# Block border of a two-block kernel: first attention round's q and k from the residual without its norm, step sizes behind the v unit

## The chip, the cores and the metric

The kernel runs on 1 core of one Trainium2 chip. The metric is the device time of one execution in microseconds (us). The engines are PE (TensorE, matmuls; PEld its weight loads), DVE (VectorE), ACT (ScalarE), POOL (GpSimd) and SP (SyncE, here only the queue of weight loads).

## The reference

Two transformer-like blocks on x of 256 rows and width 1024, all in float32. The first block ends with a feed-forward part that is added to the residual x; the second takes the norm of that sum.

```python
def first_block(x, mem, ...):
    ...
    u = _rmsnorm(x, g_mlp[l]) @ w_ff1[l]
    x = x + jnp.square(jax.nn.relu(u)) @ w_ff2[l]
    return x

def second_block(x, norm_mix_pre_w, w_in, ...):
    h = x
    u = rmsnorm(h, norm_mix_pre_w[layer])        # h * rsqrt(mean(h*h) + eps) * gain
    proj = u @ w_in[layer]
    q, k, v, z, xbc, dt_raw, gate_logits = jnp.split(proj, offsets, axis=-1)
    ... dilated window attention of q, k, v (12 heads of 64)
    ssm = mamba2_mixer(z, xbc, dt_raw, ...)      # dt = softplus(dt_raw + dt_bias)
    ...
    h = h + rmsnorm(mixed, norm_mix_post_w[layer])
    f = rmsnorm(h, norm_ffn_pre_w[layer])
    f = jnp.square(jax.nn.relu(f @ w_up[layer])) @ w_down[layer]
    h = h + rmsnorm(f, norm_ffn_post_w[layer])
    return h
```

The root mean square is one number per row of h, so (h * gain) @ w times that number is the same as the norm @ w.

## The kernel before

**Tiles.** Activations stand turned: feature on the partitions, the 256 rows along the free dimension, so a width of 1024 is 8 tiles of 128x256. Each float32 product is made of three in fp32r: an operand is split into a high part (rounded) and a low part (what is left), and `products` (L236) issues hi x hi, lo x hi, hi x lo for each of 8 tiles. A unit is 256 columns of a weight matrix: two halves of 24 matmuls each, on one PSUM bank. `x_hi` and `x_lo` hold 40 tiles of operands: `H0` is tile 0, `M0` tile 8, `Y0` tile 16; the 32 hidden tiles of the feed-forward part stand from tile `U0` = 8.

**Weight pipeline.** Three slots. SP loads a unit into `raw` when its slot's low part was made; ACT casts `raw` to `w_hi` (L198) when the unit that held the slot before has ended on PE; DVE subtracts to make `w_lo` (L204). Each engine calls `split()` by hand at places in its own program; the units are taken in order.

**Order.** Each engine has its own program, written out by hand, and waits on counters (semaphores). Nothing reorders. The stages are cross, stick, mlstm, gx, gs, gm, out, up, down, and for the second block att (3 rounds of q, k, v), ssm (8 rounds), ga, gq, out2, up2, down2.

**The border.** The down stage is `deep`: 16 units, four for each pair of output tiles. After every fourth DVE adds PSUM to `res` (L1189), ACT squares (`squares`, L642) and DVE adds the two squares of a pair (`pair`, L1135). PE sums each pair over the partitions with a matmul by ones (`norm`, L1390), four in all, after the last unit. ACT makes the inverse root (`inverse(1)`, L652, L653, into `rs_row`), DVE scales `res` by it (`scaled`, L1156), ACT makes the high part times the gain (`high`, L647), DVE the low part (`lower`, L1128), all of it on tiles `H0`. PE's q unit waits for the low parts tile by tile. DVE then makes `thin_lo` (L1208), the low part of the thin columns for the step sizes, and goes on with splits, the copies `evac` (L863) of q and k out of PSUM, and the step sizes.

**Step sizes.** `step_sizes`: PE multiplies the thin columns (L245, 24 matmuls) into bank 4; DVE adds the bias (L1212), ACT takes abs, exp, ln (L699 to L701), DVE makes dt and its running sum (L1215 to L1217). POOL writes the sums to memory for the SSM rounds. `step_columns`: PE turns the rows (L1393), DVE copies them to `dtc` and `acs` (L1221, L1222). `att_logits(0)` on PE waits for that.

Of the kernel before, what the change touches and what calls it, by code (L numbers as in the profile page):

```python
# [14 lines left out]
P = 128  # L15
# [38 lines left out]
H0, M0, Y0 = 0, 8, 16  # L54
YSB, YML, YX = Y0, Y0 + 8, Y0 + 16
# [41 lines left out]
def build(nc, a, out):  # L97

    ctx = ExitStack()
    with ctx:  # L100
# [171 lines left out]

        def rs_row():
            return cells(4096, T)
# [91 lines left out]
        def _(pool):  # L366
# [6 lines left out]
            pool.wait_ge(S("s_lo"), 4)  # L373
# [8 lines left out]
            for j in range(3):  # L382
                need(pool, "a_b", j)
                pool.dma_start(a_bias, a["att_bias"][:, 4 * j:4 * j + 4, :]).then_inc(S("a_bias"), 16)
# [7 lines left out]
        def _(act):  # L392
# [75 lines left out]
            def cross(i, j):  # L468
# [17 lines left out]
                A(rows(x_hi, 2 * j + YX, 2), bank(6, 2, T), ACT.Copy).then_inc(S("c_hi"), 1)  # L486
# [22 lines left out]
            def stick_out(j):  # L509

                act.wait_ge(S("s_y"), j + 1)
                A(rows(x_hi, 2 * j + YSB, 2), bank(7, 2, T), ACT.Copy).then_inc(S("s_hi"), 1)
# [51 lines left out]
            def mlstm_out(j):  # L564

                act.wait_ge(S("m_y"), j + 1)
                A(rows(x_hi, 2 * j + YML, 2), m_hm, ACT.Copy).then_inc(S("m_hi"), 1)
# [44 lines left out]
            def mixed(i, n):  # L612

                act.wait_ge(S("p_used"), n + 2)
                A(rows(x_hi, 2 * i + M0, 2), rows(mix, 2 * i, 2), ACT.Copy).then_inc(S("mix_hi"), 1)
# [28 lines left out]
            def high(src, g, b):  # L644

                for k in (2 * b, 2 * b + 1):
                    A(x_hi[:, H0 + k], src[:, k], ACT.Identity, scale=pc(g, k)).then_inc(S("n_hi"), 1)  # L647
# [69 lines left out]
            def att_out(j):  # L717

                act.wait_ge(S("a_y"), j + 1)
                A(rows(x_hi, 2 * j + YAT, 2), bank(7, 2, T), ACT.Copy).then_inc(S("a_hi"), 1)  # L720
# [4 lines left out]
            split()  # L725
# [52 lines left out]
            def ssm_out(j):  # L778

                act.wait_ge(S("d_yn"), j + 1)  # L780
                A(rows(x_hi, 2 * j + YSS, 2), d_y, ACT.Copy).then_inc(S("d_hi"), 1)
# [41 lines left out]
            for i in range(4):  # L823
# [3 lines left out]
                mixed(i, 16 + i)  # L827
# [22 lines left out]
        def _(dve):  # L850
# [90 lines left out]
            def cross(i, j):  # L941
# [29 lines left out]
                low(2 * j + YX, bank(6, 2, T), "c_hi", j + 1, "c_lo")  # L971
# [31 lines left out]
            for i in range(1, 4):  # L1003
# [7 lines left out]
                low(2 * (i - 1) + YSB, bank(7, 2, T), "s_hi", i, "s_lo")  # L1011
# [48 lines left out]
            def mlstm_gate(j):  # L1060
# [3 lines left out]
                low(2 * j + YML, m_hm, "m_hi", j + 1, "m_lo")  # L1064
# [822 lines left out]
```

## Time and profile before

| | us |
|---|---|
| median of 3 runs | 1271.18 |
| lowest, highest | 1270.01, 1271.70 |
| the profiled execution | 1270.2 |
| its span | 1268.4 |
| PE busy in it | 1223.2 (96%) |
| DVE busy | 809.2 (64%) |
| ACT busy | 659.8 (52%) |
| mean granted clock of PE | 0.989 |

The span runs from the first to the last instruction; the profiled execution's own time is 1.8 us longer. Busy shares are means over all stages. The page of the profile gives per line what an engine did and what ended its waits; the trace gives the same for a stretch, and each start. Matmuls overlap: one of 128x256 is shown with 0.28 us, while the next starts 0.12 us after it. A granted clock of 1.00 is 2.4 GHz, 0.50 is 1.2 GHz.

### The profile page before, as it was taken

To read this page: it belongs to the slowest core of one execution; us is meant where nothing else is said; L and a number is where in the kernel's file an instruction comes from. 1 tells how busy PE (TensorE), PEld (TensorE's weight loads), DVE (VectorE), ACT (ScalarE), POOL (GpSimd) and SP (SyncE) were. 2 spreads that over 40 slices of the span, in tenths; PEclk is the share of its full clock that TensorE was granted. 3 is DMA by queue.
4 is the path that set the end of the run, shared out by engine and by line. 5 is a ranking of instruction groups with operands and counts; after the bars stand their busy time and mean duration, and the time that the engine had idled before them with its cause. 6 is when DMAs were issued, how large, how long until landed. Compare 5 with 4: busy or idle time off the path is not lost.

```text
span 1268.4 us, 22328 instructions
## 1 busy us (share of the span) xinstructions
PE 1223.2 (96%) x9844; PEld 1197.3 (94%) x9844; DVE 809.2 (64%) x890; ACT 659.8 (52%) x764; POOL 10.4 (1%) x23
## 2 busy tenths in 40 slices
PE   7999999999999999999989999999989997999996
PEld 6999999999999999999989999999889997999996
DVE  6665666777655557774446577878874555776443
ACT  6443445677543445553334468878764444545330
POOL 0000000000000000000000000000000000000000
PEclk9999999999999999999999999999999998999998
DMA  8553454555656555556555546555446552556540
GB/s 292 168 162 105 134 163 141 146 152 165 200 172 195 166 166 166 176 190 217 182 167 164 178 118 195 167 153 160 156 156 194 194 172 67 181 185 216 183 134 34
DMA packets 210241, 210.28 MB, mean 166 GB/s; under 512 B 6476, under 2 KB 207564, under 8 KB 210144
## 3 DMA queue, kind: packets, MB, share of 16 engines
q1 hardware_dynamic: 207600, 200.30, 50.0%
q0 software_dynamic: 1968, 7.64, 2.1%
q8 instruction: 78, 1.28, 0.4%
q10 hardware_dynamic: 576, 0.90, 0.2%
q14 instruction: 19, 0.16, 0.0%
HBM read 207.73 MB, written 1.09 MB: 165 GB/s over the span
## 4 chain that ended last, share of the span: by engine, by line
PE 75%; DVE 15%; ACT 7%; issue 1%; DMA 0%; DVEq 0%; ACTq 0%
PE ps L236 68%; DVE w_lo L204 6%; PE ps L1390 5%; DVE arena L1020 4%; ACT w_hi L198 2%; DVE arena L1278 1%; ACT L404 1%; ACT arena L766 1%; PE ps L1393 1%; PE ps L245 1%; DVE res L1162 0%; DVE arena L1156 0%; ACT arena L409 0%; DVE arena L1304 0%; DVE arena L1293 0%
## 5 line engine op out<-in xcount | busy, mean ns | idle before, releaser
L236 PE MATMUL ps<-x_hi,w_hi 128*128 128x256 f32 x2752 | 791.6, 288 | 19.2 <-DVE x_lo L1128 9.0
L236 PE MATMUL ps<-x_lo,w_hi 128*128 128x256 f32 x2752 | 781.3, 284 | 0.0
L236 PE MATMUL ps<-x_hi,w_lo 128*128 128x256 f32 x2752 | 781.2, 284 | 0.0
L204 DVE TENSOR_TENSOR w_lo<-raw,w_hi 128x2048 fp32r<-128x2048 f32 x188 | 430.1, 2291 | 231.1 <-ACT w_hi L198 231.1
L236 PEld LDWEIGHTS ps<-x_hi,w_hi 128*128 128x128 f32 x2752 | 530.4, 193 | 26.8 <-issue 21.8
L236 PEld LDWEIGHTS ps<-x_lo,w_hi 128*128 128x128 f32 x2752 | 530.7, 193 | 0.8
L236 PEld LDWEIGHTS ps<-x_hi,w_lo 128*128 128x128 f32 x2752 | 530.6, 193 | 0.0
L198 ACT CAST w_hi<-raw 128x2048 fp32r<-128x2048 f32 x188 | 355.9, 1899 | 117.6 <-PE ps L236 115.6
L236 PE MATMUL ps<-w_hi,x_hi 128*128 128x256 f32 x240 | 69.1, 288 | 2.5 <-DVE w_lo L204 2.5
L1390 PE MATMUL ps<-arena 128*128 128x256 f32 (+3 forms) x448 | 68.1, 341 | 3.1 <-ACT arena L747 2.6
L236 PE MATMUL ps<-w_lo,x_hi 128*128 128x256 f32 x240 | 67.9, 283 | 0.0
L236 PE MATMUL ps<-w_hi,x_lo 128*128 128x256 f32 x240 | 67.8, 283 | 0.0
L1390 PEld LDWEIGHTS ps<-arena 128*128 128x128 f32 (+2 forms) x448 | 54.1, 169 | 11.7 <-ACT arena L747 3.6
L671 ACT ACTIVATE arena<-ps 128x512 f32<-128x512 f32 x32 | 19.1, 598 | 83.9 <-PE ps L236 83.9
L1020 DVE SCALAR_TENSOR_TENSOR arena<-arena,pcol 128x256 f32<-128x256 f32 x144 | 60.1, 480 | 3.5 <-ACT arena L527 2.7
L1390 PE MATMUL ps<-arena,cst 128*128 128x256 f32 (+1 forms) x184 | 45.2, 376 | 10.6 <-DVE arena L881 6.1
L236 PEld LDWEIGHTS ps<-w_hi,x_hi 128*128 128x128 f32 x240 | 46.0, 192 | 2.7 <-DVE w_lo L204 2.7
L1390 PEld LDWEIGHTS ps<-arena,cst 128*128 128x128 f32 x184 | 31.9, 200 | 15.8 <-issue 6.1
L236 PEld LDWEIGHTS ps<-w_hi,x_lo 128*128 128x128 f32 x240 | 46.0, 192 | 0.0
L236 PEld LDWEIGHTS ps<-w_lo,x_hi 128*128 128x128 f32 x240 | 45.9, 191 | 0.0
L1175 DVE TENSOR_TENSOR arena<-arena 128x512 f32<-128x512 f32 x32 | 22.2, 692 | 36.8 <-ACT arena L671 36.8
L609 ACT ACTIVATE arena<-ps,pcol 128x256 f32<-128x256 f32 x40 | 16.8, 471 | 49.3 <-PE ps L236 47.5
(176 smaller groups left out, 696.5 us busy)
## 6 DMA issues: line engine op xcount, KB each, us to landing
raw<-in_w_in SPq DMA_DIRECT2D x170, 512.0 KB, 4.7
raw<-in_w_ff SPq DMA_DIRECT2D x64, 512.0 KB, 4.5
raw<-in_w_up SPq DMA_DIRECT2D x32, 512.0 KB, 4.7
raw<-in_w_down SPq DMA_DIRECT2D x32, 512.0 KB, 4.4
raw<-in_w_mem_kv SPq DMA_DIRECT2D x16, 512.0 KB, 4.6
raw<-in_w_out SPq DMA_DIRECT2D x16, 512.0 KB, 4.7
raw<-in_w_ssm_proj SPq DMA_DIRECT2D x16, 512.0 KB, 4.6
raw<-in_w_x_proj SPq DMA_DIRECT2D x8, 512.0 KB, 4.5
```

The lines of the kernel that those rows point to most:

```text
L198: nc.scalar.copy(w_hi[:, s], raw[:, s]).then_inc(S(f"w_hi{s}"), 1)
L204: nc.vector.tensor_tensor(w_lo[:, s], raw[:, s], w_hi[:, s].bitcast(FP32), ALU.subtract)\
L236: last = nc.tensor.matmul(dst, l, r, start=start and k == 0 and m == 0, stop=stop and k == nk - 1 and m == 2)
L245: last = nc.tensor.matmul(dst, wt[:, c], xt[:, at + k, :], start=k == 0 and m == 0, stop=k == KT - 1 and m == 2)
L404: act.preload_act_table_set("natural_log_exp_and_others")
L609: last = A(gt[:, c], unit_bank(u)[:, c], ACT.Sigmoid, bias=pc(b_gate, k + c))
L671: A(f, unit_bank(u), ACT.Relu).then_inc(taken(u), 1)
L766: A(d_ec, d_ec, ACT.Exp, scale=-1.0).then_inc(S("d_e"), 1)
L1020: last = stt(dst[:, n], pad[:, n, m:m + T], pc("conv_w" + name, tiles[n] + stride * m), dst[:, n], ALU.mult, ALU.add)
L1175: chain(tt(q, f, bc(rs_row(), 2), ALU.mult))
L1278: tt(d_ec, d_ec, bc(d_cb, 4), ALU.mult).then_inc(S("d_L"), 1)
L1390: return nc.tensor.matmul(o, l, r, start=start, stop=stop)
```

## The change

- In the down stage ACT and DVE also make, after each quarter, the high and low part of the residual times the second block's gain (`high` and `lower` on `res`, tiles `H0`, counters `b_hi`, `b_lo`).
- PE runs the first half of q of the first round on those, then the four sums of squares, the second half of q, and k. q and k come out of PSUM by a multiplication with `rs_row` where they were copied (two `tt` in place of two `evac`).
- The normed parts go to tiles `H2` = 8 and are read from the v unit on. The mixed sums of the second block stand at `M2` = 0 in turn.
- PE's thin products for the step sizes stand between the halves of v, in bank 7; the turning of the step columns between the halves of the next round's q. The wait for the columns goes from the first logits to the first `att_values`.
- On ACT and DVE the split of the v unit stands ahead of the inverse norm and of the scaling. On POOL the first bias table is loaded ahead of the step rows, when the low parts are done.
- The counters of five stages become one pair, `y_hi` and `y_lo`.

DVE from the end of the down stage to the first scaling, before (a quarter's addition is L1189, the pair L1135, the scaling L1156) and after (the same are L1199, L1145, L1166; L205 is `split`):

```order
L1189 TENSOR_TENSOR res<-res,ps 128x512
L1135 TENSOR_TENSOR arena<-arena 128x256
L1156 TENSOR_TENSOR arena<-res,arena 128x512 x2
L1128 SCALAR_TENSOR_TENSOR x_lo<-arena,pcol,x_hi 128x256 x2
L1156 TENSOR_TENSOR arena<-res,arena 128x512
```

```order
L1199 TENSOR_TENSOR res<-res,ps 128x512
L1138 SCALAR_TENSOR_TENSOR x_lo<-res,pcol,x_hi 128x256 x2
L1145 TENSOR_TENSOR arena<-arena 128x256
L205 TENSOR_TENSOR w_lo<-raw,w_hi 128x2048
L1166 TENSOR_TENSOR arena<-res,arena 128x512 x2
L1138 SCALAR_TENSOR_TENSOR x_lo<-arena,pcol,x_hi 128x256 x2
```

Two low parts of the residual and the subtraction of the v unit's weights now stand ahead of the scaling.

DVE from the thin low part to the first logits, before (L863 is `evac`, L1212 to L1217 `step_sizes`, L1221 and L1222 `step_columns`, L1228 the logits' bias) and after (`evac` of q and k is now L1262; `step_sizes` L1225 to L1230; bias L1241):

```order
L1208 TENSOR_TENSOR x_lo<-tab,x_hi 128x320
L204 TENSOR_TENSOR w_lo<-raw,w_hi 128x2048
L863 COPY arena<-ps 128x512
L204 TENSOR_TENSOR w_lo<-raw,w_hi 128x2048
L1212 TENSOR_SCALAR mix<-ps,tab 32x256
L1215 SCALAR_TENSOR_TENSOR mix<-mix 32x256
L1216 TENSOR_SCALAR mix<-mix,small 32x256
L1217 SCALAR_TENSOR_TENSOR mix<-mix 32x256
L863 COPY arena<-ps 128x512
L204 TENSOR_TENSOR w_lo<-raw,w_hi 128x2048
L1221 COPY small<-ps 128x64
L1222 COPY small<-ps 128x64
```

```order
L1221 TENSOR_TENSOR x_lo<-tab,x_hi 128x320
L1262 TENSOR_TENSOR arena<-ps,arena 128x512 x2
L205 TENSOR_TENSOR w_lo<-raw,w_hi 128x2048 x2
L1225 TENSOR_SCALAR mix<-ps,tab 32x256
L1228 SCALAR_TENSOR_TENSOR mix<-mix 32x256
L1229 TENSOR_SCALAR mix<-mix,small 32x256
L1230 SCALAR_TENSOR_TENSOR mix<-mix 32x256
L1241 SCALAR_TENSOR_TENSOR arena<-ps,arena 128x1536
```

Both evacuations and two splits stand ahead of the step sizes, one split went ahead of the scaling, and the column copies went behind the logits.

ACT across the same border, before (L642 square, L652 and L653 inverse root, L647 high parts, L198 split) and after (L652, L662 and L663, L657, L199):

```order
L198 CAST w_hi<-raw 128x2048 x4
L642 ACTIVATE arena<-res 128x512
L652 ACTIVATE arena<-ps,small 128x256
L653 ACTIVATE arena<-arena 128x256
L647 ACTIVATE x_hi<-arena,pcol 128x256 x8
```

```order
L199 CAST w_hi<-raw 128x2048 x4
L657 ACTIVATE x_hi<-res,pcol 128x256 x2
L652 ACTIVATE arena<-res 128x512
L199 CAST w_hi<-raw 128x2048
L662 ACTIVATE arena<-ps,small 128x256
L663 ACTIVATE arena<-arena 128x256
L657 ACTIVATE x_hi<-arena,pcol 128x256 x8
```

The v unit's cast stands between the square and the inverse root.

The diff, cut to its core:

```diff
 H0, M0, Y0 = 0, 8, 16
+H2, M2 = M0, H0
...
+            def bias(j):
+
+                need(pool, "a_b", j)
+                pool.dma_start(a_bias, a["att_bias"][:, 4 * j:4 * j + 4, :]).then_inc(S("a_bias"), 16)
+
+            pool.wait_ge(S("n_lo"), 2 * KT)
+            bias(0)
             pool.wait_ge(S("dt_rows"), 1)
...
-            def deep(dst, done0, stop):
+            def deep(dst, done0, stop, g=None):
...
                         act.wait_ge(S(f"deep{b // 4 % 2}"), b // 8 + done0 + 2)
+                        if g is not None:
+                            high(dst, g, b // 4, H0, "b_hi")
                         squares(dst, b // 4 * 2)
 
             hidden("up", 0)
-            deep(res, 0, 16)
-
-
+            deep(res, 0, 16, "norm_mix_pre_w_2")
+            split()
             inverse(1)
             for b in range(4):
                 act.wait_ge(S("n_t"), b + 1)
-                high(cells(2048, KT, T), "norm_mix_pre_w_2", b)
+                high(cells(2048, KT, T), "norm_mix_pre_w_2", b, H2)
...
             split()
             split()
             step_sizes()
-            split()
             evac(U("att", 0, 2, 3), a_v)
...
                         last.then_inc(S(f"deep{c % 2}"), 1)
+                        if g is not None:
+                            lower(dst, g, c, 0, H0, ("b_hi", "b_lo"))
                         pair(n, c)
...
-            split()
-            evac(U("att", 0, 0, 3), a_q)
+            for n, dst in enumerate((a_q, a_k)):
+                u = U("att", 0, n, 3)
+                finished(dve, u)
+                tt(dst, unit_bank(u), bc(rs_row(), 2), ALU.mult).then_inc(taken(u), 1)
+            split()
             split()
             step_sizes()
-            evac(U("att", 0, 1, 3), a_k)
-            split()
-            step_columns()
             for i in (1, 2):
                 att_logits(i - 1)
                 split()
+                if i == 1:
+                    step_columns()
                 evac(U("att", i, 0, 3), a_q)
...
-            for b in range(4):
-                norm(1, b)
-
...
-                if j == 0:
-                    pe.wait_ge(S("dt_col"), 1)
...
             q, k, v = (U("att", 0, n, 3) for n in range(3))
-            unit(q, H0, lo=("n_lo", KT, 1))
+            half(q, 0, H0, lo=("b_lo", 0, 1))
+            for b in range(4):
+                norm(1, b)
+            half(q, 1, H0)
+            unit(k, H0)
+            half(v, 0, H2, TOK, lo=("n_lo", KT, 1))
             step_sizes()
-            unit(k, H0)
-            half(v, 0, H0, TOK)
-            step_columns()
-            half(v, 1, H0, TOK)
+            half(v, 1, H2, TOK)
             for i in (1, 2):
                 q, k, v = (U("att", i, n, 3) for n in range(3))
                 att_logits(i - 1)
-                unit(q, H0)
-                unit(k, H0)
-                half(v, 0, H0, TOK)
+                half(q, 0, H2)
+                if i == 1:
+                    step_columns()
+                half(q, 1, H2)
+                unit(k, H2)
+                half(v, 0, H2, TOK)
                 att_turn(i - 1)
-                half(v, 1, H0, TOK)
+                half(v, 1, H2, TOK)
+                if i == 1:
+                    pe.wait_ge(S("dt_col"), 1)
                 att_values(i - 1)
```

## Rows read from the trace of the kernel before

**Rows 1.** PE's waits by releaser, 470 to 680 us: total us, times, longest.

```profile
PE ps L236 <- DVE x_lo L1128: 2.9, 1, 2.9
```

**Rows 2.** timeline of PE at the border: start us, us, engine line op, count.

```profile
658.34 0.28 PE L236 MATMUL ps<-x_hi,w_lo 128*128 128x256 f32 x1
658.46 1.46 PE L1390 MATMUL ps<-arena,cst 128*128 128x256 f32 x6
660.52 0.70 PE L1390 MATMUL ps<-arena,cst 128*128 128x256 f32 x2 [0.60 <-DVE arena L1135]
664.11 0.55 PE L236 MATMUL ps<-x_hi,w_hi 128*128 128x256 f32 x1 [2.89 <-DVE x_lo L1128]
...
669.30 0.28 PE L236 MATMUL ps<-x_hi,w_lo 128*128 128x256 f32 x1
...
672.28 0.28 PE L245 MATMUL ps<-x_hi 128*32 128x256 f32 x1
...
675.08 0.28 PE L236 MATMUL ps<-x_hi,w_hi 128*128 128x256 f32 x1
...
683.80 0.43 PE L1393 MATMUL ps<-cst,mix 32*128 32x32 f32 x4
...
687.23 1.68 PE L1390 MATMUL ps<-arena 64*128 64x128 f32 x16
...
703.34 1.36 PE L1393 MATMUL ps<-cst,arena 128*128 128x128 f32 x11
```

**Rows 3.** busy time by stretch: PE, PEld, DVE, ACT, POOL, then granted clock, DMA.

```profile
664.10:668.00 3.90, 3.89 (x17) 3.86 (x18) 3.90 (x10) 3.05 (x9) 0.00 (x0) 0.50 0.00 0
```

**Rows 4.** timeline of DVE at the border, columns as in PE's.

```profile
654.88 2.29 DVE L204 TENSOR_TENSOR w_lo<-raw,w_hi 128x2048 fp32r<-128x2048 f32 x1 [3.47 <-ACT w_hi L198]
658.66 0.69 DVE L1189 TENSOR_TENSOR res<-res,ps 128x512 f32<-128x512 f32 x1 [1.48 <-PE ps L236]
...
662.21 1.29 DVE L1156 TENSOR_TENSOR arena<-res,arena 128x512 f32<-128x512 f32 x2 [1.75 <-ACT arena L653]
...
668.42 0.49 DVE L1208 TENSOR_TENSOR x_lo<-tab,x_hi 128x320 fp32r<-128x320 f32 x1
...
676.69 0.47 DVE L1212 TENSOR_SCALAR mix<-ps,tab 32x256 f32<-32x256 f32 x1
...
679.43 0.68 DVE L1217 TENSOR_TENSOR_SCAN mix<-mix 32x256 f32<-32x256 f32 x1
...
696.57 1.83 DVE L1239 TENSOR_TENSOR arena<-arena,small 128x512 f32<-128x512 f32 x2
```

**Rows 5.** timeline of ACT in the down stage: one high part of a weight unit.

```profile
652.95 1.90 ACT L198 CAST w_hi<-raw 128x2048 fp32r<-128x2048 f32 x1 [3.86 <-PE ps L236]
```

**Rows 6.** timeline at the out stage's end: DVE, then ACT, then PE.

```profile
468.33 0.68 DVE L1145 TENSOR_TENSOR res<-res,ps 128x512 f32<-128x512 f32 x1
469.59 0.89 DVE L1128 SCALAR_TENSOR_TENSOR x_lo<-res,pcol,x_hi 128x256 fp32r<-128x256 f32 x2 [0.58 <-ACT x_hi L647]
470.51 0.42 DVE L1135 TENSOR_TENSOR arena<-arena 128x256 f32<-128x256 f32 x1
...
469.05 0.91 ACT L647 ACTIVATE x_hi<-res,pcol 128x256 fp32r<-128x256 f32 x2 [2.96 <-DVE res L1145]
...
466.93 0.60 PE L1390 MATMUL ps<-arena,cst 128*128 128x256 f32 x2
...
467.48 0.28 PE L236 MATMUL ps<-x_lo,w_hi 128*128 128x256 f32 x1
```

**Rows 7.** timeline of PE in the last SSM round, after a wait.

```profile
924.65 0.36 PE L236 MATMUL ps<-x_hi,w_hi 128*128 128x256 f32 x1 [3.57 <-DVE w_lo L204]
...
925.36 0.42 PE L236 MATMUL ps<-x_hi,w_lo 128*128 128x256 f32 x1
...
928.57 0.33 PE L236 MATMUL ps<-x_hi,w_lo 128*128 128x256 f32 x1
```

**Rows 8.** transfers by line, 640 to 760 us: size, median us to landing.

```profile
arena<-in_att_bias POOLq DMA_DIRECT2D x3, 768.0 KB, 4.7
```

More of the change, by code:

```diff
@@ L381, in _ @@
             pool.wait_ge(S("dt_out"), 16)
-            for j in range(3):
-                need(pool, "a_b", j)
-                pool.dma_start(a_bias, a["att_bias"][:, 4 * j:4 * j + 4, :]).then_inc(S("a_bias"), 16)
+            for j in (1, 2):
+                bias(j)
             pool.wait_ge(S("a_t"), 3)
@@ L485, in cross @@
                 act.wait_ge(S("c_y"), j + 1)
-                A(rows(x_hi, 2 * j + YX, 2), bank(6, 2, T), ACT.Copy).then_inc(S("c_hi"), 1)
+                A(rows(x_hi, 2 * j + YX, 2), bank(6, 2, T), ACT.Copy).then_inc(S("y_hi"), 1)
                 if i < 4:
@@ L511, in stick_out @@
                 act.wait_ge(S("s_y"), j + 1)
-                A(rows(x_hi, 2 * j + YSB, 2), bank(7, 2, T), ACT.Copy).then_inc(S("s_hi"), 1)
+                A(rows(x_hi, 2 * j + YSB, 2), bank(7, 2, T), ACT.Copy).then_inc(S("y_hi"), 1)
             for i in range(1, 4):
@@ L566, in mlstm_out @@
                 act.wait_ge(S("m_y"), j + 1)
-                A(rows(x_hi, 2 * j + YML, 2), m_hm, ACT.Copy).then_inc(S("m_hi"), 1)
+                A(rows(x_hi, 2 * j + YML, 2), m_hm, ACT.Copy).then_inc(S("y_hi"), 1)
             split()
@@ L610, in gate, with mixed @@
                 last.then_inc(taken(u), 1)
-            def mixed(i, n):
+            def mixed(i, n, at=M0):
                 act.wait_ge(S("p_used"), n + 2)
-                A(rows(x_hi, 2 * i + M0, 2), rows(mix, 2 * i, 2), ACT.Copy).then_inc(S("mix_hi"), 1)
+                A(rows(x_hi, 2 * i + at, 2), rows(mix, 2 * i, 2), ACT.Copy).then_inc(S("mix_hi"), 1)
             def gated(stage, i, k, n, b_gate="b_gate"):
@@ L719, in att_out @@
                 act.wait_ge(S("a_y"), j + 1)
-                A(rows(x_hi, 2 * j + YAT, 2), bank(7, 2, T), ACT.Copy).then_inc(S("a_hi"), 1)
+                A(rows(x_hi, 2 * j + YAT, 2), bank(7, 2, T), ACT.Copy).then_inc(S("y_hi"), 1)
             split()
@@ L780, in ssm_out @@
                 act.wait_ge(S("d_yn"), j + 1)
-                A(rows(x_hi, 2 * j + YSS, 2), d_y, ACT.Copy).then_inc(S("d_hi"), 1)
+                A(rows(x_hi, 2 * j + YSS, 2), d_y, ACT.Copy).then_inc(S("y_hi"), 1)
             att_exps(2)
@@ L970, in cross @@
                 split()
-                low(2 * j + YX, bank(6, 2, T), "c_hi", j + 1, "c_lo")
+                low(2 * j + YX, bank(6, 2, T), "y_hi", j + 1, "y_lo")
                 if i == 4:
@@ L1074, in _ @@
             split()
-            low(6 + YSB, bank(7, 2, T), "s_hi", 4, "s_lo")
+            low(6 + YSB, bank(7, 2, T), "y_hi", 8, "y_lo")
             mlstm_conv(0)
@@ L1178, in hidden, with deep @@
                     low(2 * c + U0, q, "f_hi", c + c0 + 1, "f_lo")
-            def deep(stage, dst, add, n, stop):
+            def deep(stage, dst, add, n, stop, g=None):
                 for b in range(16):
@@ L1194, in _ @@
             hidden("up", 0)
-            deep("down", res, True, 1, 16)
+            deep("down", res, True, 1, 16, "norm_mix_pre_w_2")
+            split()
             nt = cells(2048, KT, T)
@@ L1280, in ssm_skip @@
             def ssm_skip(j):
-                need(dve, "d_lo", j)
+                if j:
+                    dve.wait_ge(S("y_lo"), j + 15)
                 for c in range(2):
@@ L1307, in ssm_low @@
             def ssm_low(j):
-                low(2 * j + YSS, d_y, "d_hi", j + 1, "d_lo")
+                low(2 * j + YSS, d_y, "y_hi", j + 16, "y_lo")
             att_logits(2)
@@ L1598, in _, with gated @@
                 half(o, 1, H0)
-            def gated(stage, i, at, nk=KT):
-                unit(U(stage, i, 0, 2), H0)
+            def gated(stage, i, at, nk=KT, h=H0):
+                unit(U(stage, i, 0, 2), h)
                 unit(U(stage, i, 1, 2), at, FP, nk)
-            pe.wait_ge(S("c_lo"), 4)
+            pe.wait_ge(S("y_lo"), 4)
             gated("gx", 0, YX)
@@ L1666, in step_columns @@
                     for t in range(2):
-                        last = tr(bank(5, 2, 2, 32)[:, n, t], row[:, t * P:(t + 1) * P])
+                        last = tr(dt_columns()[:, n, t], row[:, t * P:(t + 1) * P])
                 last.then_inc(S("dt_ct"), 1)
@@ L1749, in _ @@
             att_logits(2)
-            unit(x, H0)
-            unit(b_c, H0)
-            half(z, 0, H0)
+            unit(x, H2)
+            unit(b_c, H2)
+            half(z, 0, H2)
             att_turn(2)
-            half(z, 1, H0)
+            half(z, 1, H2)
             att_values(2)
```

66 lines of the change are left out of this document (34 added, 32 removed).

## The prediction

> **What bounds the kernel now.** The page's table of engines comes first: PE is busy for 1223.2 of 1268.4 us, so time can only be won where PE stands still or runs slowly. The reader then looks at the table of waits, cut to the stretch of the change: between 470 and 680 us PE waits long for one thing only, the x_lo tiles of the block border [rows 1]. The timeline of PE shows how that wait lies in the order of work. The last product of the first block is issued at 658.34, eight matmuls of the sum of squares follow in two groups, and the first product of the attention's q unit starts at 664.11, after 2.89 us of standing [rows 2]. All of that stretch is one chain through DVE, ACT and PE: add, square, pair, sum, logarithm and exponential, scaling, split.
>
> The third view is the granted clock by stretch: it is 0.50 from 664.1 to 668.0 [rows 3], the 1.2 GHz level, behind that standstill. The starts say what this costs. From 664.11 to 669.30 there are 23 products, 0.226 us each; from 669.30 to 672.28 there are 25, 0.119 us each [rows 2]. So the border costs PE both the gap and the slow restart. From 672.28 on PE runs without a wait until past the first turn at 703.34 (the table of waits has no line for PE between 680 and 760 us).
>
> **The stretch that is compared.** It goes from 658.46, when the last product is out, to the start of the first logits at 687.23, 28.77 us [rows 2]. In it: sum and wait 5.65, q unit 8.17, step-size products 2.80, k unit and first half of v 8.72, turning of the step columns and second half of v 3.43. Behind it nothing is changed in kind.
>
> **PE's new sequence, term by term.** Half a unit is 24 products at 0.12, 2.88 us, a pitch that the rows from 669.30 to 672.28 show.
> - First half of q: 2.88, from 658.46 to 661.34. It reads the residual times the gain, no norm; six of its eight tiles are old, and only 6 and 7 come from the last addition.
> - Sum of squares: 8 matmuls. Six took 1.46 us, that is 0.243 each, so 1.95 [rows 2]. At the end of the out stage a pair among products took 467.48 - 466.93 less one product, 0.43, so four pairs 1.72 [rows 6]. I take 1.95, from the same place and the same grouping, and keep 1.72. Before, this work was hidden in the wait; now it is on PE's path.
> - Second half of q 2.88, k 5.76, first half of v 2.88, step-size products 2.80, second half of v 2.88.
>
> The sum is 22.03. The turning of the step columns, 3.43 - 2.88 = 0.55 with its switch, goes behind the first half of the next q and is still paid. 28.77 - 22.03 - 0.55 = **6.19 us less**. The same from the other side: 5.65 - 1.95 = 3.70 of gap, 8.17 - 5.76 = 2.41 of slow clock, and 0.08 from k and v.
>
> **Is tile 7 there in time?** The out stage already does this very chain on the residual (add, two high parts, two low parts, square, pair), so its offsets can be carried over. From the start of the add, the two low parts start at 1.26 and end at 2.15, and the pair ends at 2.60 [rows 6]. The border's add starts at 658.66 [rows 4]. So tile 6 is ready at about 660.37 and tile 7 at 660.81; PE asks at 658.46 + 18 x 0.12 = 660.62 and at 660.98. The pair is ready at 661.26 and PE asks at 661.34. All three hold, by 0.25, 0.17 and 0.08 us. That is thin, but missing by x costs x and no more: a gap of a few tenths. I take 0 and keep 0.5 as the bound.
>
> **The second half of the chain.** It now runs beside the rest of q and k. The sum ends on PE at 661.34 + 1.95 = 663.29; from the sum's end (661.22) to the first scaling (662.21) it was 0.99 [rows 2, 4], so 664.28. But DVE has the v unit's low part ahead of it. ACT is free for v's high part when the square is done, 2.18 behind the add [rows 6], at 660.84; 1.90 for the cast [rows 5] and 2.29 for the subtraction [rows 4] give 665.03. That is later than 664.28, so it decides. From the first scaling to the end of the thin low parts took 668.91 - 662.21 = 6.70 [rows 4], which gives 671.73. PE asks for the first normed tile of v at 663.29 + 2.88 + 5.76 = 671.93, and the last tile of eight is asked for 2.5 us later. It holds, with 0.20 even if the thin parts are counted in, which v's first half does not need.
>
> **Step sizes and evacuation.** The two evacuations of q and k become multiplications by the norm's row. The trace has a two-operand operation on 128x512 from PSUM, the add at 658.66, 0.69 us [rows 4]. I count both whole, though two copies go: 671.73 to 673.3, k's end waited for. Behind them stand two low parts (2 x 2.29) to 677.9, then comes the step chain, which took from 676.69 to 680.11, 3.42 [rows 4]: to 681.3. The logits start on PE at 658.46 + 22.03 = 680.49 and take 1.68 [rows 2], and DVE is wanted at 682.2. Nine tenths of a microsecond are left. If that cover went, ACT's and DVE's softmax work would slide, which has 703.34 - 698.40 = 4.9 us to the turn [rows 2, 4]. POOL's first bias table is no longer queued behind the step rows: it is issued when the last low part is out, near 671, and lands 4.7 us later [rows 8], well ahead of 682; the row table that it was ahead of is wanted only in the SSM rounds. The queue of SP is not reordered; v's slot comes free at 665.0 instead of 671.9, so its next load is earlier.
>
> **The added work in the down stage.** Three times before the border ACT has 0.91 and DVE 0.89 more [rows 6] in front of the next splits. A slot's low part is finished 657.17 - 652.95 = 4.2 us after the unit that held it ended [rows 4, 5], and is wanted two units, 11.5 us, after. 7.3 us of cover against at most 1.8 and the 1.8 of the add and square that are there already: nothing. The merged counters of the other stages keep their order and move nothing.
>
> **The skill against the rows.** After a 3.57 us wait in the last SSM round PE restarted fast, fell to the slow pitch at 925.36 and came back near 928.57: 15 gaps in 3.21 us, 0.214 each, so 15 x 0.094 = 1.4 us lost [rows 7]. At the border 2.4 us were lost behind a wait of much the same length. So the price of the same gap is not a constant of the kernel. The Trainium skill, page "TensorE: Matmul & The Clock Gate", section "Part 1: The HAM clock gate", says that the clock's transition is not tied to the kernel's start and that the number of slow matmuls differs between runs of one kernel. This trace agrees as far as the two places differ. By it this execution's 2.4 is one draw: with 1.4 drawn here, the sum would be 5.2. The clock rival below is worked out from the rows alone.
>
> **How the profile stands to the median.** The profiled execution took 1270.2 us, its span is 1268.4. The median of the runs is 1271.18, 1.0 above. 1270.2 - 6.2 = 1264.0; from the median 1265.0, which is my forecast.
>
> **The rivals.**
> 1. Whole gain, 6.2 (range 5.7 to 6.5 with the bounds above): 1264.7 to 1265.5, give or take the half microsecond by which runs differ. Chance 0.70.
> 2. A link of the chain is late: tiles 6 and 7, the pair, or v's low part pushing the scaling past v's first half. For: covers of 0.08 to 0.25 us, and 0.20. Against: each offset is measured at a twin place. If v's turn slips by a whole pair of scaled tiles, 1.5 us, and the early tiles by 0.5, the time is 1267.2. Chance 0.13.
> 3. The clock falls elsewhere, or not where it did. Everything behind the border meets the same waits 6.2 us earlier. One slow stretch more costs 1.4 to 2.4 [rows 2, 7], one less gives as much: 1262.6 to 1263.6, or 1266.4 to 1267.4. For: the two unequal losses. Against: the three runs before differ by 1.7 us in all. Chance 0.11. The page of the Trainium skill named above would make this rival the common case.
> 4. The gain is eaten downstream: the SSM rounds, where DVE and ACT are on the chain, take the earlier start and give 4 to 6 of it back in a wait. Against: the att rounds in between run PE without a wait, so PE alone sets the phase at which the SSM starts. Then it is 1269 to 1271. Chance 0.04.
> 5. Slower: the added casts in the down stage hold back the splits. ACT and DVE stand in order, so the next low part comes later by what is ahead of it; PE waits once this is over 7.3 us, at four places. For a loss of all 6.2 and 3 more, 9.2 us in four places, each would have to be late by 9.6 us. The rows put it at 3.6. That gives 1274. Chance 0.02.
>
> **The numbers.** A measurement of this kernel tells about 0.2%, 2.5 us, from no change: the bound is 1268.64. Cases 1 to 3 lie below it. The forecast is case 1's, 1265.0. Cases 1, 2 and 3 lie between 1262.6 and 1267.4; with what the estimates may miss at either edge this leaves out 1 to 2 in 10. Faster 0.93, same 0.05, slower 0.02.
>
> **What would show it.** Right: no wait of PE for x_lo at the border; granted clock 1.00 from 655 to 700; eight sum matmuls behind 24 products; 22 us from the last down product to the first logits. Wrong in a step: a wait in front of tile 6 or 7 or of the pair; a wait at v's first half with DVE's v subtraction in front of it; DVE's step chain ending after 682 and the logits' bias addition late; a new wait for w_lo in the down stage. The SSM rounds should show the waits for w_lo that they had, and no others.

## The result and the profile after

The changed kernel takes 1264.04 us (median of 5 runs, 1263.21 to 1265.56), the kernel before 1271.18 (median of 5, 1269.26 to 1271.70). The ratio is 0.9948, 95% interval 0.9934 to 0.9963: 0.5% faster, 4.7 to 8.4 us. The forecast was 1265.0.

The profiled execution of the changed kernel is its slowest run, 1265.56 us with a span of 1263.8, so the two profiles are only 4.6 us apart. The page's line for the engines:

```profile
PE 1222.2 (97%) x9844; PEld 1197.5 (95%) x9844; DVE 812.5 (64%) x898; ACT 662.9 (52%) x772; POOL 10.5 (1%) x23
```

PE is as busy as before (1223.2) in a shorter span: what went is standing time. PE's timeline at the border, in the columns of [rows 2]; L1406 are the sums of squares and, from 681.19, the logits; L246 the step-size products; L1409 the turns:

```profile
659.20 0.28 PE L237 MATMUL ps<-x_hi,w_lo 128*128 128x256 f32 x1
...
662.19 1.03 PE L1406 MATMUL ps<-arena,cst 128*128 128x256 f32 x4
...
663.73 0.47 PE L237 MATMUL ps<-x_hi,w_hi 128*128 128x256 f32 x1
664.03 0.28 PE L237 MATMUL ps<-x_lo,w_hi 128*128 128x256 f32 x1
...
675.43 0.28 PE L246 MATMUL ps<-x_hi 128*32 128x256 f32 x1
...
678.22 0.28 PE L237 MATMUL ps<-w_hi,x_hi 128*128 128x256 f32 x1
...
681.19 0.72 PE L1406 MATMUL ps<-arena 64*128 64x128 f32 x6
...
685.86 0.43 PE L1409 MATMUL ps<-cst,mix 32*128 32x32 f32 x4
...
697.85 1.36 PE L1409 MATMUL ps<-cst,arena 128*128 128x128 f32 x11
```

The last product of the first block starts at 659.20, the first of q 0.12 later, at 659.32 (below this is the free point: the start of whatever comes next on PE), and nothing stands still until the logits at 681.19. From 659.32 that is 21.87 us, where [rows 2] had 28.77. The sum of squares, four matmuls in the program that the trace shows as eight (the prediction counts the eight), takes 663.73 - 662.19 = 1.54, and the first product behind it holds the next one up: 0.30 from 663.73 to 664.03, where 0.12 is usual. Up to the first turn, with the step columns at 685.86 now inside, it is 697.85 - 659.32 = 38.53 against 703.34 - 658.46 = 44.88: 6.35 us less.

DVE's timeline over the same stretch, to be read against [rows 4]. L1199 is the add, L1138 the low parts, L1145 the pair, L205 the v unit's subtraction, L1166 the scaling, L1221 the thin low part, L1225 to L1230 the step chain:

```profile
659.52 0.69 DVE L1199 TENSOR_TENSOR res<-res,ps 128x512 f32<-128x512 f32 x1 [1.48 <-PE ps L237]
660.78 0.89 DVE L1138 SCALAR_TENSOR_TENSOR x_lo<-res,pcol,x_hi 128x256 fp32r<-128x256 f32 x2 [0.58 <-ACT x_hi L657]
661.70 0.43 DVE L1145 TENSOR_TENSOR arena<-arena 128x256 f32<-128x256 f32 x1
663.50 2.29 DVE L205 TENSOR_TENSOR w_lo<-raw,w_hi 128x2048 fp32r<-128x2048 f32 x1 [1.37 <-ACT w_hi L199]
665.70 1.29 DVE L1166 TENSOR_TENSOR arena<-res,arena 128x512 f32<-128x512 f32 x2
...
671.91 0.49 DVE L1221 TENSOR_TENSOR x_lo<-tab,x_hi 128x320 fp32r<-128x320 f32 x1
...
678.42 0.47 DVE L1225 TENSOR_SCALAR mix<-ps,tab 32x256 f32<-32x256 f32 x1 [0.43 <-PE ps L246]
...
681.18 0.68 DVE L1230 TENSOR_TENSOR_SCAN mix<-mix 32x256 f32<-32x256 f32 x1
```

And the busy times (PE, PEld, DVE, ACT, POOL), granted clock, DMA share and GB/s from 655 to 700 us; the clock was 0.50 in [rows 3]:

```profile
655.00:700.00 45.00, 45.00 (x374) 43.90 (x373) 32.28 (x41) 22.11 (x42) 1.65 (x3) 1.00 0.61 191
```

**Where the profile's other 1.7 us went.** 6.35 less 4.6 leaves 1.7: this execution lost 0.86 before the border (the add is at 659.52, not 658.66) and 0.9 behind it (565.06 us from the first turn to the end before, 565.95 after). Slow stretches of the clock account for both. The busy times at 22 to 28 us and behind the 3.57 us wait of [rows 7], of the kernel before:

```profile
22.00:28.00 6.00, 5.87 (x48) 5.81 (x48) 6.00 (x12) 2.74 (x5) 0.00 (x0) 1.00 0.64 190
921.00:932.00 11.00, 7.43 (x49) 7.30 (x48) 7.67 (x8) 8.32 (x9) 0.00 (x0) 0.84 0.21 72
```

of the changed kernel:

```profile
22.00:28.00 6.00, 6.00 (x39) 6.00 (x39) 6.00 (x11) 2.58 (x5) 0.00 (x0) 0.72 0.63 193
915.00:926.00 11.00, 7.43 (x43) 7.26 (x42) 7.64 (x8) 8.61 (x9) 0.00 (x0) 0.69 0.21 72
```

PE runs with 0.72 of the clock where it had 1.00, in code that the change does not touch, and with 0.69 behind the wait where it had 0.84. It is the same code and the same wait (3.57 us in both). From the restart behind that wait (924.65 and 919.19) to the restart behind the 5.01 us wait ahead of the up2 stage (1061.30 and 1056.22) the changed kernel needs 0.38 us more. From there to the restart behind the last long wait (1259.12 and 1254.48) it needs 0.44 more; the clock of the first 12 us is 0.66 there, against 0.70.

### The profile page after: what moved, and what is told of

Read it like the earlier page. It is cut to its first block, busy times and chain, and to the rows that moved or that the text cites. A ratio compares the mean times of both kernels' runs of the same rounds, so it can differ in the third digit from the quotient of the medians.

```text
span 1263.8 us, 22345 instructions
## 1 busy us (share of the span) xinstructions
PE 1222.2 (97%) x9844; PEld 1197.5 (95%) x9844; DVE 812.5 (64%) x898; ACT 662.9 (52%) x772; POOL 10.5 (1%) x23
## 4 chain that ended last, share of the span: by engine, by line
PE 76%; DVE 15%; ACT 7%; issue 1%; DMA 0%; DVEq 0%; ACTq 0%
PE ps L237 69%; DVE w_lo L205 5%; PE ps L1406 5%; DVE arena L1030 4%; ACT w_hi L199 2%; DVE arena L1293 1%; ACT L414 1%; ACT arena L776 1%; PE ps L1409 1%; PE ps L246 1%; DVE res L1172 1%; ACT arena L419 0%; DVE arena L1166 0%; DVE arena L1309 0%; DVE x_lo L883 0%
## 5 line engine op out<-in xcount | busy, mean ns | idle before, releaser
L205 DVE TENSOR_TENSOR w_lo<-raw,w_hi 128x2048 fp32r<-128x2048 f32 x188 | 430.1, 2291 | 227.3 <-ACT w_hi L199 227.2
L199 ACT CAST w_hi<-raw 128x2048 fp32r<-128x2048 f32 x188 | 355.8, 1899 | 110.1 <-PE ps L237 107.6
L1406 PE MATMUL ps<-arena 128*128 128x256 f32 (+3 forms) x448 | 68.1, 341 | 3.1 <-ACT arena L757 2.7
L1406 PEld LDWEIGHTS ps<-arena 128*128 128x128 f32 (+2 forms) x448 | 54.1, 169 | 11.7 <-ACT arena L757 3.7
L1406 PE MATMUL ps<-arena,cst 128*128 128x256 f32 (+1 forms) x184 | 44.9, 375 | 10.1 <-DVE arena L891 6.2
L1406 PEld LDWEIGHTS ps<-arena,cst 128*128 128x128 f32 x184 | 32.0, 200 | 14.8 <-issue 6.2
```

Source lines behind the costliest of these rows:

```text
L199: nc.scalar.copy(w_hi[:, s], raw[:, s]).then_inc(S(f"w_hi{s}"), 1)
L205: nc.vector.tensor_tensor(w_lo[:, s], raw[:, s], w_hi[:, s].bitcast(FP32), ALU.subtract)\
L1406: return nc.tensor.matmul(o, l, r, start=start, stop=stop)
```

## Experiments

**The changed kernel again.** No edit.

> The changed kernel once more, unaltered. The main theory (the border's standstill and slow restart are gone, nothing else moved): again about 21.9 us from the last down product to the first logits, no wait of PE between 470 and 760 us, median 1263.5 to 1265. The clock theory (the price of one and the same gap is drawn anew in each execution): the waits of PE are the same as in the first profile of this kernel to 0.2 us, but the slow stretches behind them are not: the one behind the 3.57 us wait, which was 1.9 us of lost time in one profile and over 3 in another, has another length, and the slow stretch at 22 to 28 us may be missing. If instead the clock falls in the same places for the same time, the clock theory is wrong and the difference of 0.9 us that the first profile had before the border needs another cause.

Measured: 1264.37 us (1263.80 to 1265.15), ratio 0.9950 (0.9938 to 0.9963). The same two stretches:

```profile
22.00:28.00 6.00, 5.68 (x47) 5.69 (x48) 6.00 (x11) 2.93 (x5) 0.00 (x0) 1.00 0.63 190
915.00:926.00 11.00, 7.46 (x49) 7.31 (x48) 7.67 (x8) 8.26 (x9) 0.00 (x0) 0.84 0.21 72
```

The clock is 1.00 at 22 to 28 us and 0.84 behind the wait. The first product of q starts at 658.63, the sum of squares at 661.51, the first turn at 697.16: 38.53 us from the first product to the turn, as in the first profile. This profile's execution took 1263.92, 6.28 below the profile of before, 6.35 of it at the border. So the stretch takes the changed kernel the same time in both executions, and the slow stretches elsewhere are drawn anew. The 6.35 holds against this one profile of the kernel before: a run below shows that the old border, too, has a shorter slow stretch at times.

**The gap filled, in the kernel before.**

```diff
-            for b in range(4):
-                norm(1, b)
+            begin(U("att", 0))
+            pe.wait_ge(S("deep0"), 3)
+            for b in range(4):
+                if b == 3:
+                    filler(5, U("att", 0), bank(3, T))
+                norm(1, b)
+            filler(22, U("att", 0), bank(3, T))
```

> The kernel before, with 27 more products on PE inside the border's standstill (5 while it waits for the last pair, 22 while it waits for the normed tiles), written to a PSUM bank that nobody reads; their results are not used. The gap stays, only PE is at work in it. Main theory: the gap's length and the clock are two terms, 3.7 and 2.4 us. Then the wait for x_lo stays in place, filled, the granted clock stays 1.00 from 655 to 672, the q unit takes 5.8 instead of 8.2 us, and the time is 2.4 us less than before: 1268.8. Rival (the slow stretch comes from the tiles arriving one by one, or the clock falls whatever PE does there): q unit still about 8 us and the time 1271.

Measured: 1269.70 us (1269.41 to 1271.62) against 1270.70, ratio 0.9997 (0.9988 to 1.0006). The times don't separate them. The trace does. PE's timeline at q's first tiles, the first step-size product, and the busy times and clock of 664.1 to 668.0:

```profile
664.09 0.36 PE L236 MATMUL ps<-x_hi,w_hi 128*128 128x256 f32 x1 [0.27 <-DVE x_lo L1128]
...
665.39 0.38 PE L236 MATMUL ps<-x_hi,w_hi 128*128 128x256 f32 x1 [0.36 <-DVE x_lo L1128]
...
666.79 0.39 PE L236 MATMUL ps<-x_hi,w_hi 128*128 128x256 f32 x1 [0.37 <-DVE x_lo L1128]
...
671.30 0.28 PE L245 MATMUL ps<-x_hi 128*32 128x256 f32 x1
...
664.10:668.00 3.90, 3.17 (x21) 2.76 (x22) 3.90 (x10) 3.06 (x9) 0.00 (x0) 1.00 0.00 0
```

The clock is at 1.00, as the theory said. But q takes 671.30 - 664.09 = 7.21 us, not 5.8. With a fast clock PE has done a pair of tiles in 0.7 us, and the next pair comes from DVE after 1.3 to 1.4 (664.09, 665.39, 666.79), so PE waits in front of each. From the free point, 658.42, to the logits, 686.25, it is 27.83 us against 28.77: **0.94 us is what the slow clock cost here**, not 2.4. The other 1.45 is the pace of DVE's scaling and low parts, which stood hidden behind the slow products.

**Only q from the residual.**

```diff
             half(q, 1, H0)
-            unit(k, H0)
-            half(v, 0, H2, TOK, lo=("n_lo", KT, 1))
+            unit(k, H2, lo=("n_lo", KT, 1))
+            half(v, 0, H2, TOK)
```

(and DVE copies k as before).

> The changed kernel, but only q is made from the residual without its norm; k reads the normed tiles. Main theory (the second half of the chain is covered by q and k together, not by q alone): PE asks for k's first tile 7.3 us after the last down product and its low part is there about 0.8 later, then the tiles come at 0.72 us each against 0.36 that PE needs, so PE waits about 2.3 us in all at k and the time is 1266.4. Rival (q alone would have covered it, k's part of the change is worth nothing): 1264, no wait at k.

Measured: 1266.36 us (1266.10 to 1267.20), ratio 0.9966 (0.9954 to 0.9979). PE's timeline:

```profile
661.25 1.89 PE L1405 MATMUL ps<-arena,cst 128*128 128x256 f32 x8
...
666.67 0.36 PE L237 MATMUL ps<-x_hi,w_hi 128*128 128x256 f32 x1 [0.66 <-DVE x_lo L1138]
...
667.97 0.39 PE L237 MATMUL ps<-x_hi,w_hi 128*128 128x256 f32 x1 [0.36 <-DVE x_lo L1138]
...
669.37 0.39 PE L237 MATMUL ps<-x_hi,w_hi 128*128 128x256 f32 x1 [0.38 <-DVE x_lo L1138]
...
682.53 1.68 PE L1405 MATMUL ps<-arena 64*128 64x128 f32 x16
```

Three waits in front of k's tiles, at the pace just seen. From the sum of squares to the logits 682.53 - 661.25 = 21.28 us, against 680.50 - 661.51 = 18.99 in the changed kernel: 2.29 more, as expected. k is needed as cover.

**v's split where it was.** ACT's and DVE's `split()` of the v unit back behind the thin low part.

```diff
             deep("down", res, True, 1, 16, "norm_mix_pre_w_2")
-            split()
...
             tt(thin_lo, tab[:, 0:40 * KT], thin_hi.bitcast(FP32), ALU.subtract).then_inc(S("thin_lo"), 1)
+            split()
```

> The changed kernel, but ACT's and DVE's split of the v unit stands where the kernel before had it, behind the thin low part. Main theory (v's weights must be split ahead of the scaling, since PE reaches v 13 us after the last down product): DVE's scaling starts about 1.3 us earlier, v's low part is done about 15.1 us after the last down product and PE waits about 2 us for w_lo at v; behind it the q and k evacuations and the step chain are later but still covered. Time 1266.2, 2 above the changed kernel. Rival (v's split is hidden either way, its new place is worth nothing): 1264.2, no wait for w_lo between 660 and 700 us.

Measured: 1266.84 us (1266.18 to 1269.03), ratio 0.9972 (0.9961 to 0.9982). DVE's subtraction for v, and PE's first product of v and the logits:

```profile
671.40 2.29 DVE L205 TENSOR_TENSOR w_lo<-raw,w_hi 128x2048 fp32r<-128x2048 f32 x1 [0.67 <-ACT w_hi L199]
...
673.80 0.36 PE L237 MATMUL ps<-w_hi,x_hi 128*128 128x256 f32 x1 [2.13 <-issue]
...
682.49 1.68 PE L1406 MATMUL ps<-arena 64*128 64x128 f32 x16
```

v's low part is done at 673.69 and PE starts at 673.80 after 2.13 us (the profile names no releaser, but the next event before it is the end of that subtraction). From the sum of squares to the first turn it is 699.15 - 661.15 = 38.00 against 697.16 - 661.51 = 35.65: 2.35 more. Without this move a third of the gain is gone. One detail was expected too large: DVE's scaling starts 664.03 - 661.15 = 2.88 behind the sum of squares, against 665.03 - 661.51 = 3.52, so v's subtraction holds it up by 0.6 us and not 1.3.

**The step columns ahead of the first logits, as before.**

```diff
+                if i == 1:
+                    step_columns()
+                    pe.wait_ge(S("dt_col"), 1)
                 att_logits(i - 1)
                 half(q, 0, H2)
-                if i == 1:
-                    step_columns()
                 half(q, 1, H2)
```

> The changed kernel, but the step columns are turned and copied ahead of the first logits, and the logits wait for them, as in the kernel before. Main theory (the step chain ends on DVE about as late as the logits start, so the turning had to move): PE waits 0.6 us for the step rows, turns for 0.4, and the logits start 0.3 later, behind the copies: 1.1 to 1.4 us more from the last down product to the first turn. Time 1265.4. Rival (the place of the columns does not matter): the stretch is unchanged within 0.2 and the time 1264.3.

Measured: 1266.24 us (1265.52 to 1266.53), ratio 0.9963 (0.9950 to 0.9975). PE's timeline, turn of the columns, logits, first turn of the weights:

```profile
681.09 0.43 PE L1408 MATMUL ps<-cst,mix 32*128 32x32 f32 x4 [0.67 <-DVE mix L1230]
...
681.97 1.68 PE L1405 MATMUL ps<-arena 64*128 64x128 f32 x16 [0.45 <-DVE small L1235]
...
698.07 1.47 PE L1408 MATMUL ps<-cst,arena 128*128 128x128 f32 x12
```

(On DVE the copies of the columns move ahead of the logits in the same way.) PE waits 0.67 for the step rows and 0.45 for the copies. From the sum of squares to the first turn it is 698.07 - 661.36 = 36.71 against 35.65: 1.06 more. The medians are 1.9 apart, from runs on different occasions; the ratios' intervals overlap. In this profile the clock behind the long wait of the SSM rounds was 0.69 over 11 us, as in the slowest run of the changed kernel; that is a part of it. The stretch says 1.06, just under the 1.1 to 1.4 expected, and I go by that.

**The squares first.**

```diff
+                        squares(dst, b // 4 * 2)
                         if g is not None:
                             high(dst, g, b // 4, H0, "b_hi")
-                        squares(dst, b // 4 * 2)
```

> The changed kernel, but at each quarter of the down stage ACT makes the squares ahead of the two high parts of the residual, so the last high and low parts come about 0.55 us later. Main theory (the first half of q covers the last tiles by 0.25 and 0.17 us, the pair by 0.06; what misses, costs what it misses by): tile 6 is 0.3 late, tile 7 0.1 on top of that, the pair about 0.1, together 0.4 to 0.6 us more from the last down product to the first logits; in the total 1264.3 to 1264.9. Rival (a link of the chain that is late restarts PE slowly, or the norm slides past v): 1.5 us or more in the same stretch.

Measured: 1265.35 us (1263.44 to 1265.50), ratio 0.9956 (0.9943 to 0.9968). PE's timeline:

```profile
658.30 0.28 PE L237 MATMUL ps<-x_hi,w_hi 128*128 128x256 f32 x1
...
660.83 0.39 PE L237 MATMUL ps<-x_hi,w_hi 128*128 128x256 f32 x1 [0.21 <-DVE x_lo L1138]
...
680.68 1.68 PE L1406 MATMUL ps<-arena 64*128 64x128 f32 x16
```

PE waits in front of tile 6 (660.83, where 660.46 was due), and this half of q takes 3.39 us (658.30 to 661.69) in place of 2.88. From 658.30 to the logits 22.38 us, against 21.87: 0.51 more, inside the 0.4 to 0.6 expected. The median is 1.0 above that of the run "again", over the 0.6; the ranges overlap. A late link cost what it was late by; no slow clock followed.

**Only the added work.** The kernel before, with `high` and `lower` on the residual in the down stage, their results read by nobody.

```diff
-            deep("down", res, True, 1, 16)
+            deep("down", res, True, 1, 16, "norm_mix_pre_w_2")
```

(the same on ACT, which also waits for the last of these low parts before the inverse root).

> The kernel before with only the added work of the change in the down stage: ACT and DVE make the high and low parts of the residual times the gain after each quarter; nobody reads them, the normed parts overwrite them. Main theory: at the first three quarters they cost nothing (over 5 us of cover for the next split); at the border they stand between the addition and the pair, which ends 2.6 instead of 1.8 us behind the addition, so the stretch from the last down product to the first logits is 0.8 longer, and so is the time: 1271.5 to 1271.9 against 1271.1. Rival (the added casts delay the splits in the down stage): a wait of PE for w_lo between 560 and 655 us, and over 2 us more in all.

Measured: 1270.66 us (1269.98 to 1272.33) against 1270.71, ratio 1.0003 (0.9994 to 1.0012). PE has no wait between 470 and 660 us, so the added parts cost nothing at the first three quarters. At the border, PE's timeline:

```profile
658.26 1.46 PE L1395 MATMUL ps<-arena,cst 128*128 128x256 f32 x6
...
661.12 0.70 PE L1395 MATMUL ps<-arena,cst 128*128 128x256 f32 x2 [1.40 <-DVE arena L1138]
664.77 0.36 PE L236 MATMUL ps<-x_hi,w_hi 128*128 128x256 f32 x1 [2.95 <-DVE x_lo L1131]
...
672.49 0.28 PE L245 MATMUL ps<-x_hi 128*32 128x256 f32 x1
...
687.44 1.68 PE L1395 MATMUL ps<-arena 64*128 64x128 f32 x16
```

The pair ends 0.8 later and q starts 664.77 - 658.26 = 6.51 after the last product is out, against 5.65 in [rows 2]. Yet the logits come after 29.18 us, only 0.41 later: q takes 7.72 where it took 8.17, for the clock was slow for about half as long this time (0.79 on average from 662 to 670 us, against 0.57 in the kernel before). The total's 0.8 was not seen; it drowns in such draws.

**Kept at work in three later gaps.** The changed kernel with fillers.

```diff
             half(b_c, 1, YAT, FP, 6)
+            filler(26, H2, bank(7, T))
             gated("ga", 1, YAT, 6, H2)
...
+            begin(U("up2", 0))
+            pe.wait_ge(S("q_proj"), 5)
+            filler(5, 39, bank(3, T))
             norm(2, 3)
+            filler(56, 39, bank(3, T))
             half(U("up2", 0), 0, H0, lo=("n_lo", 2 * KT, 1))
...
+            evacuated(pe, U("up2", 15))
             for b in range(4):
+                if b == 3:
+                    filler(5, 39, unit_bank(U("up2", 15))[:, 0])
                 norm(4, b)
+            filler(54, 39, unit_bank(U("up2", 15))[:, 0])
```

> The changed kernel with 26, 61 and 59 more products on PE inside three later standstills (the 3.6 us wait in the ga stage, the block's inner norm before the up2 stage, the last norm before the output), written to PSUM banks that nobody reads; their results are not used. Clock theory: each of these waits keeps its length, and the products behind it start at 0.12 instead of 0.21 us: 1.4 to 3 us less at the first, about 1 at the second, 0.5 to 1 at the third, together 3 to 5: 1259.5 to 1261. Rival (the products behind the second and third gap are paced by DVE, and the fillers overrun the gaps): 1262.5 to 1265.

Measured: 1262.92 us (1262.51 to 1263.59), ratio 0.9940 (0.9927 to 0.9952). Busy times and clock at the first two gaps, with fillers:

```profile
900.00:930.00 30.00, 27.21 (x217) 26.32 (x216) 23.06 (x30) 23.91 (x31) 0.00 (x0) 1.00 0.37 118
1050.00:1066.00 16.00, 14.96 (x114) 14.14 (x113) 12.48 (x25) 8.39 (x15) 0.00 (x0) 1.00 0.01 2
```

and in the changed kernel without them (the run "again"):

```profile
900.00:930.00 30.00, 25.59 (x192) 24.71 (x191) 23.03 (x31) 23.91 (x31) 0.00 (x0) 0.94 0.38 117
1050.00:1066.00 16.00, 9.90 (x55) 9.01 (x54) 12.46 (x25) 8.37 (x15) 0.00 (x0) 0.68 0.01 3
```

The clock goes from 0.94 and 0.68 to 1.00 in both. The medians are 1.45 us apart, half or less of the 3 to 5 expected, and the time lies in the rival's range. PE's restart behind the first gap and its next wait, without fillers and with them:

```profile
918.59 0.36 PE L237 MATMUL ps<-x_hi,w_hi 128*128 128x256 f32 x1 [3.54 <-DVE w_lo L205]
...
926.31 0.36 PE L237 MATMUL ps<-x_hi,w_hi 128*128 128x256 f32 x1 [0.24 <-DVE w_lo L205]
```

```profile
926.34 0.36 PE L237 MATMUL ps<-x_hi,w_hi 128*128 128x256 f32 x1 [1.74 <-DVE w_lo L205]
```

With the clock at 1.00 PE is done with these products sooner, and then waits 1.74 us in place of 0.24 for the next unit's low part. It goes on at the same time, so the first filler gave nothing. Against the run "again", DVE's work lies 0.65 us earlier behind the second gap and 1.02 at the end of the program, so the second filler brought about 0.65 and the third about 0.4 in these two profiles. The 1.4 us that the prediction reads as lost in [rows 7] were most likely hidden in the same way; fillers were tried at this place in the changed kernel alone.

**The order at the end of the SSM rounds.** The 3.57 us wait of [rows 7] is of the same kind as v's split: weights whose slot is long free, their split queued behind something that waits.

```diff
             ssm_inputs(7)
-            ssm_mask(7)
             split()
+            ssm_mask(7)
             ssm_scale(6)
+            split()
             ssm_low(6)
             ssm_skip(7)
-            split()
```

(on ACT the first split goes behind `ssm_silu(7)`, the second behind `ssm_norm(6)`).

> The changed kernel with one thing more, at the end of the SSM rounds: ACT's split of the first weights of gated unit 1 stands behind silu(7) in place of behind decay(7), the next one behind the inverse norm, and DVE's in the same order. Theory: PE's 3.6 us wait for w_lo is not work but order, a split queued behind the decay; its slot has been free for over 10 us. Then the wait is under 1 us, and its slow stretch goes with it: 3 to 5 us less, 1259.5 to 1261. Rival: the next unit's weights are late instead, and the wait moves on by one unit: within 1 us of the changed kernel, 1263.5 to 1264.5.

Measured: 1257.72 us (1257.63 to 1258.65), ratio 0.9898 (0.9885 to 0.9912). PE's waits for w_lo between 895 and 960 us and the last sum of squares of the SSM rounds, in the changed kernel (the run "again"):

```profile
PE ps L237 <- DVE w_lo L205: 4.4, 3, 3.5
...
942.46 1.03 PE L1406 MATMUL ps<-arena,cst 128*128 128x256 f32 x4
```

and with the new order:

```profile
PE ps L237 <- DVE w_lo L205: 0.6, 1, 0.6
...
936.94 1.03 PE L1410 MATMUL ps<-arena,cst 128*128 128x256 f32 x4
```

The waits fall from 4.4 to 0.6 us. From the first turn to that sum it is 936.94 - 697.40 = 239.54 us against 942.46 - 697.16 = 245.30: 5.76 less. That is more than the 3.8 us of waits: with the next unit's weights early as well, the time that the slow stretch cost PE comes back too (the clock is 1.00 from 909 to 930 us). It is nearly as much as the whole border, and more than the 3 to 5 us expected; the medians are 6.32 and 6.65 below the two of the changed kernel.

**With fillers on top.** The same, with the second and third filler of the run above.

> The kernel of the run before in this set, with products whose results are not used on PE in the standstill before the up2 stage (61) and before the output (59). Theory: the two gaps keep their length, the clock stays at 1.00 through both, and because most of what follows the first is paced by DVE's tiles, both together give no more than the 1.5 us that three fillers gave: 1 to 1.5 us below the kernel without them. Rival: nothing within 0.3 us.

Measured: 1257.06 us (1256.74 to 1257.75), ratio 0.9892 (0.9879 to 0.9906), 0.66 below the kernel without fillers; the ranges overlap (1257.63 to 1258.65 without). That is less than the theory's 1 to 1.5 and more than the rival's 0.3; between the two profiles it is 0.36. It is the fastest of the kernels run, 1.1% under the kernel before.

## Why the prediction was right

**The total.** 1264.04 against 1265.0. The stretch gave 6.35 (again in the second profile) where 6.19 were summed up. The two medians are 7.1 apart, 0.8 more than the stretch; in the later set of runs they are 6.3 apart (1270.70 and 1264.37), so that 0.8 lies within the scatter of the runs.

**The terms on PE.** Half a unit at 2.87 and 2.88 and the step-size products at 2.79 came out as put. The sum of squares was mis-sized: 1.72 for 1.95, that is 1.54 to the next start and 0.18 by which the first product behind it holds up the second. The second half of q and k therefore take 8.82 and not 8.64. The 1.95 was worked out as 8 x 1.46 / 6 from [rows 2], but 1.46 is the time to the shown end of the last one, which overlaps what comes next. The lower bound, 1.72 from [rows 6], is what came: the pair there has the same delay behind it. The second half of v took 2.97, 0.09 over, up to the logits. Together 2.87 + 1.54 + 8.82 + 2.88 + 2.79 + 2.97 = 21.87. The columns cost (697.85 - 681.19) - (703.34 - 687.23) = 0.55, as put.

**Tiles 6 and 7 and the pair.** Offsets from the out stage held to 0.01: low parts at 1.26 and ended at 2.15, the pair ended at 2.61 behind the add. PE took no wait. That the covers are as thin as said, and that a miss costs its own length, `sqfirst` shows: 0.51 us for low parts that start 1.79 behind the add in place of 1.26.

**The second half of the chain.** v's split decided, as put: scaling at 665.70, 6.38 us behind the free point 659.32, where 6.57 was worked out; thin parts done 13.08 behind it (13.27 worked out), v's first product 13.23 (13.47). `vlate` and `qonly` show that both legs are needed, 2.35 and 2.29 us.

**Step sizes.** The chain ended at 681.86, 22.54 behind the free point (22.8 put), and DVE's next work, the logits, came 1.1 later. `cols` shows what the cover is worth: 1.06.

**The added work.** Nothing in the down stage, shown by `addonly` and by the absence of waits in the changed kernel.

**The step that was wrong, though the sum was right,** is the split of the gain in two: "3.70 of gap" and "2.41 of slow clock". The second was 8.17 less an unhindered q unit. `fill` shows that with the clock at full speed q still takes 7.21, because DVE delivers tiles slower than PE uses them. So the slow clock's share was 0.94, and 1.45 were the tiles' pace. Three executions bear this out: q took 8.17, 7.72 (`addonly`) and 7.21 (`fill`) with ever less slow clock. The sum was not touched, for the change takes away both; that is luck as far as the split goes. The same slip gave too high a price to rival 3 and to the expectation of `warm`. Two smaller slips: the waits that the prediction calls "much the same length" are 2.89 and 3.57 us, and rival 2's 1.5 and 0.5 on top of 1265.0 make 1267.0, not 1267.2.

**The rivals.** Rival 3, another draw of the clock, did come in the first profile (1.7 us lost against the profile of before), and not in the second; in the medians, 1264.04 and 1264.37, it does not show. Rivals 2, 4 and 5 did not come: no wait at the border, the SSM rounds' waits as they were, no late split in the down stage. The sentence with the Trainium skill, page "TensorE: Matmul & The Clock Gate", section "Part 1: The HAM clock gate", that the number of slow matmuls differs between runs, is borne out: the same code at 22 to 28 us ran at 1.00, 0.72 and 1.00 in three profiles. What the page's rule was used for, a sum of 5.2, was wrong by the step above: with the shorter slow stretch of `addonly`, where q took 0.45 less, the stretch would have given 5.9, an estimate from 6.35 and 0.45.

## What to carry to other kernels

A factor that is one number per row can be left out of a product's input and applied on its output; this takes a whole reduction off the path if the work between covers it, and the cover must be counted for each later consumer, here 13 us for v. When an engine restarts slowly behind a wait, don't book all of its slow time to the clock: fill the gap with work that nobody reads, and see what paces it then. It can be the next wait, as at the first filler of `warm`, and then the slow clock costs nothing. And look in each engine's queue for work whose inputs are long ready behind work that still waits: moving v's split was worth 2.35 of the 6.3 us, and moving two splits at the end of the SSM rounds another 5.8.

## What the runs showed of the hardware

- A float32 matmul of the sum of squares (128x256) is shown as two records. Four of them together cost 1.54 us to the next start and 0.18 more behind it (changed kernel); one alone among the products costs 0.43 with the same delay, 4 x 0.43 = 1.72 by [rows 6]. Taking them together saved nothing.
- A wait of 3.54 to 3.57 us on PE was followed by a stretch at half clock of twice the length in one execution as in another of the same program: a clock of 0.69 over 11 us is 6.8 us at half speed, 0.84 is 3.5.
- What such a stretch costs depends on what paces PE behind it. The border's cost 0.94 us (`fill`). The shorter one in the SSM rounds cost nothing (`warm`), since PE would have waited for the next weights. Fillers kept the clock at 1.00 through three gaps of 3.5 us and more, for 1.45 us in the medians.
